# One VectorE instruction instead of two for the low parts of four chunks of a pair group

## The reference

```python
x = x + 0.5 * _swiglu(_rmsnorm(x, ffn1_norm), w_gate1, w_up1, w_down1)
u = _rmsnorm(x, mix_norm) @ w_in            # attention of two kinds on u
x = x + concat([a_out, b_out]) @ w_out
x = x + 0.5 * _swiglu(_rmsnorm(x, ffn2_norm), w_gate2, w_up2, w_down2)
x = _rmsnorm(x, final_norm)

def _swiglu(x, w_gate, w_up, w_down):
    return (silu(x @ w_gate) * (x @ w_up)) @ w_down
```

## Time and profile before

| | |
|---|---|
| median of three runs | 1835.73 us |
| the profiled execution, its own time | 1836.09 us |
| its span, first to last instruction | 1834.0 us |
| mean granted TensorE clock | 0.997 |
| TensorE matmul busy | 1819.8 us (99%) |
| TensorE weight load busy | 1511.5 us (82%) |
| VectorE busy | 1268.5 us (69%) |
| ScalarE busy | 922.6 us (50%) |
| GpSimd busy | 21.6 us (1%) |

### The profile page before, as it was taken

The page is one execution under the profiler, slowest core; times in us unless marked ns, Lnnn a source line. Parts: engine busy times, 40 slices in busy tenths (PEclk is TensorE's granted clock), DMA queues, the critical chain, the costliest instruction groups (busy, mean ns, idle before and its releaser), DMA issues.

```text
span 1834.0 us, 22446 instructions
## 1 busy us (share of the span) xinstructions
PE 1819.8 (99%) x8356; PEld 1511.5 (82%) x8356; DVE 1268.5 (69%) x1473; ACT 922.6 (50%) x1148; POOL 21.6 (1%) x19
## 2 busy tenths in 40 slices
PE   9999999999999999999999999999999999999998
PEld 7888888887888888888888888888888888888887
DVE  7888555887456868666666566888545887656865
ACT  7554434554344545554666445554434554344554
POOL 0000000000000000100000000000000000000000
PEclk9999999999999999999999999999999999999998
DMA  9565655556655657655554466565655556565653
GB/s 337 199 216 195 216 185 190 197 196 229 217 188 169 223 170 240 215 167 171 169 188 161 156 221 230 200 214 196 216 190 185 197 196 243 203 220 195 220 171 113
DMA packets 233792, 366.99 MB, mean 200 GB/s; under 512 B 16240, under 2 KB 94832, under 8 KB 233712
## 3 DMA queue, kind: packets, MB, share of 16 engines
q1 hardware_dynamic: 232224, 364.05, 59.4%
q10 hardware_dynamic: 1488, 1.87, 0.3%
HBM read 346.85 MB, written 2.10 MB: 190 GB/s over the span
## 4 chain that ended last, share of the span: by engine, by line
PE 95%; DVE 2%; DMA 1%; SPq 1%; ACT 0%; issue 0%; POOL 0%; DVEq 0%; ACTq 0%
PE psum L1804 74%; PE psum L1845 8%; PE psum L1717 7%; PE psum L1722 3%; DVE w_split L1189 1%; SPq L463 0%; DMA w_raw<-in_ffn_gate 0%; DMA w_raw<-in_ffn_down 0%; DMA w_raw<-in_ffn_up 0%; DVE strip_sum L1231 0%; DVE squares L1223 0%; PE psum L1964 0%; PE psum L1975 0%; PE psum L2010 0%; PE psum L1990 0%
## 5 line engine op out<-in xcount | busy, mean ns | idle before, releaser
L1804 PE MATMUL psum<-w_split,x_split 128*128 128x512 f32 x3984 | 915.9, 390 | 0.5 <-DVE w_split L1048 0.5
L1804 PEld LDWEIGHTS psum<-w_split,x_split 128*128 128x128 f32 x3984 | 746.9, 188 | 157.8 <-DVE w_split L1048 1.3
L606 ACT ACTIVATE w_split<-w_raw 128x1024 fp32r<-128x1024 f32 (+1 forms) x404 | 416.3, 1043 | 463.7 <-PE psum L1804 394.3
L1048 DVE TENSOR_TENSOR w_split<-w_raw,w_split 128x1024 fp32r<-128x1024 f32 (+1 forms) x404 | 477.7, 1203 | 241.7 <-ACT w_split L606 239.8
L1804 PE MATMUL psum<-w_split,h_split 128*128 128x512 f32 x2208 | 503.7, 390 | 1.6 <-DVE w_split L1189 1.2
L1804 PEld LDWEIGHTS psum<-w_split,h_split 128*128 128x128 f32 x2208 | 413.8, 188 | 89.7 <-DVE w_split L1189 2.6
L717 ACT ACTIVATE w_split<-w_raw 128x1024 fp32r<-128x1024 f32 (+1 forms) x320 | 319.3, 1013 | 280.8 <-PE psum L1804 189.9
L1189 DVE TENSOR_TENSOR w_split<-w_raw,w_split 128x1024 fp32r<-128x1024 f32 (+1 forms) x320 | 362.1, 1162 | 75.0 <-ACT w_split L717 73.8
L1845 PE MATMUL psum<-w_split,pair_sums 128*128 128x512 f32 x384 | 102.4, 395 | 0.0
L1845 PEld LDWEIGHTS psum<-w_split,pair_sums 128*128 128x128 f32 x384 | 72.1, 188 | 17.4
L1717 PE MATMUL psum<-x_split,w_split 128*128 128x512 f32 x256 | 79.9, 396 | 0.0
(11 more groups left out here) (211 smaller groups left out, 905.4 us busy)
## 6 DMA issues: line engine op xcount, KB each, us to landing
w_raw<-in_ffn_down SPq DMA_DIRECT2D x76, 1024.0 KB, 5.6
w_raw<-in_ffn_up SPq DMA_DIRECT2D x71, 1024.0 KB, 5.4
w_raw<-in_ffn_gate SPq DMA_DIRECT2D x70, 1024.0 KB, 5.4
w_raw<-in_w_in SPq DMA_DIRECT2D x48, 512.0 KB, 5.1
w_raw<-in_w_in SPq DMA_DIRECT2D x24, 1024.0 KB, 5.2
w_raw<-in_ffn_gate SPq DMA_DIRECT2D x34, 512.0 KB, 4.0
w_raw<-in_ffn_up SPq DMA_DIRECT2D x32, 512.0 KB, 4.8
w_raw<-in_w_out SPq DMA_DIRECT2D x16, 1024.0 KB, 5.4
```

Source lines behind the costliest of these rows:

```text
L606: nc.scalar.activation(w_split[:, slot % 2, 0, h * half:(h + 1) * half], w_raw[:, slot, h * half:(h + 1) * half], ACT.Copy).then_inc(hi_ma ...
L1048: nc.vector.tensor_tensor(w_split[:, slot % 2, 1, part], w_raw[:, slot, part], w_split[:, slot % 2, 0, part].bitcast(F32), ALU.subtract).t ...
L1804: ins = mm(psum[:, bank + t, :], x[:, a, t * P:(t + 1) * P], w[:, b, k, :], start=kk == 0 and (a, b) == (0, 0) and t in begins, stop=kk == ...
```

## The change

Inside `seven_low`, for jobs 8 to 11, the loop over two halves is replaced by one wait for the second half's high copy and one subtraction over all of the chunk (2048 elements; 1536 in the third part of the second stage for jobs 10 and 11, where the chunks are smaller). It adds 2 to `lo_made` when it ends. Jobs 2 to 7, the high copies, and all waits of other engines are as before.

```diff
                 kind, raw = SEVEN_JOBS[n]
                 c, slot, half = seven_base(ph, i) + n, raw % 4, kn * STRIP // 2
+                if n >= 8:
+                    dve.wait_ge(hi_made, hi_value(c, 1))
+                    nc.vector.tensor_tensor(w_split[:, n % 2, 1, 0:2 * half], w_raw[:, slot, 0:2 * half],
+                                            w_split[:, n % 2, 0, 0:2 * half].bitcast(F32), ALU.subtract).then_inc(lo_made, 2)
+                    return
                 for h, part in enumerate((slice(0, half), slice(3 * half // 2 if kind == "blocks" else half, 2 * half))):
                     dve.wait_ge(hi_made, hi_value(c, h))
                     nc.vector.tensor_tensor(w_split[:, n % 2, 1, part], w_raw[:, slot, part], w_split[:, n % 2, 0, part].bitcast(F32),
                                             ALU.subtract).then_inc(lo_made, 1)
```

## The result

The changed kernel takes 1861.81 us (median of 4 runs, 1861.6 to 1862.01) against 1835.9 us before (median of 4 runs too): a ratio of 1.0141, 95% interval [1.0128, 1.0154], 25.9 us slower. The forecast was 1861.8.

The account below looks back on a forecast made before the run. The matmul engine, busy 99%, was taken as the bound, VectorE mattering only by when it hands over chunks. Added waits of 22.5 + 3.2 + 0.5 - 0.1 = 26.1 us gave 1861.8 us; range 1857 to 1866, widened to 1853 to 1867.

Parts of the forecast that it names:

- VectorE's time is worth nothing: Matmul engine busy 99%, VectorE 69%: saved VectorE time gains nothing; only when it hands TensorE a chunk matters.
- The duration: One wide subtraction of 2048 elements on VectorE takes 2.285 us, against 2.36 for two halves.
- The chain of job 8, gates, silu and job 9: In each pair group gates and silu come 0.88 us late; TensorE waits 1.41 on average for job 9, 22.5 in all.
- Jobs 10 and 11: Job 10 covered by 2.4 us; job 11 at ends of parts 1 and 2: three groups 3.2 us, the fourth 0.5.
- Part 3's ends: In part 3's last groups the hidden columns TensorE waits for come 0.07 us earlier, twice: -0.1 us.
- the sum: All terms together, 22.5 + 3.2 + 0.5 - 0.1: 26.1 us slower, 1861.8 us on the median.
- B: Rival, 6%: gates not pushed, only the direct wait for the whole of job 9 counts, plus the ends: 1847.8 us.
- C: Rival, 3%: the granted clock falls to 1.2 GHz after some stalls, one plain job per pair group at half speed: 1948 us.
- D: Rival, 3%: the wide instruction is cheap, 2048 elements running at a higher rate than 1024; nothing slower, 1834 to 1836 us.
- E: Rival, 4%: unseen cover makes TensorE's waits shorter than the chain says; within 0.2%, about 1837 us.

Follow-up runs that it names:

- e11: Kernel before, with part-3 hidden columns first, half of job 11 ahead of the ups (but one group), jobs 8 to 10 wide, job 9's copy before silu: 1833.76 us.
- e5_job11: Kernel before, with only job 11's low part as one wide instruction: 1839.30 us, ratio 1.0019.
- e7_silu_last: Changed kernel, with the second high half of job 9 moved ahead of silu on ScalarE: 1838.98 us, ratio 1.0018.
- e3_jobs89: Kernel before, with the low parts of jobs 8 and 9 wide, jobs 10 and 11 in halves: 1858.83 us, ratio 1.0131.
- e4_job10: Kernel before, with only job 10's low part as one wide instruction: 1836.67 us, ratio 1.0004.
- e2_job9: Kernel before, with only job 9's low part as one wide instruction: 1843.37 us, ratio 1.0042.

## Why the prediction was right, step by step

**VectorE's time is worth nothing.** Right, by the changed kernel and by e11.

**The duration.** 2.285 us was forecast by the line through two shapes; 2.288 came (2.25 to 2.29). The Trainium skill's formula, page "VectorE: DVE Perf Modes", gives 2.29 too; the trace agrees.

**The chain of job 8, gates, silu and job 9.** Right, and shown from four sides: job 8 alone 0, job 9 alone 8.0, both 23.4, and nothing left of it with silu moved. The gates were forecast 4.6 us after job 7's first load and came at 80.31 - 75.67 = 4.64; silu 7.8, came 7.88. The wait was forecast with 1.41 on average. The sixteen add up to 26.05 us as the profile gives idle time; each holds the 0.04 us that always lies between two loads, so 1.59 each. 0.14 of that are the two starts of a wide instruction 0.07 later than I had put them. But the loads behind a wait run closer, 72 of them in 16.19 to 16.23 us where the same 72 take 16.28 without one, so that the net is the 1.53 us above. 16 x 1.53 = 24.4 us, forecast 22.5. What did not come as written is the order of the groups: the one at 1480 us was to have the smallest wait, 1.25, and has 1.70; the smallest, 1.42, is at 1201 us. How far ahead of the gates job 7 starts goes by the landing of the transfer that job 8's high copy waits for: in the group at 1480 us this copy starts 0.04 us after job 7's first load before, and 0.29 after. So the average carried over, and the single group did not.

**Jobs 10 and 11.** Right: three waits of 1.40 (forecast 0.34 + 1.07 = 1.41), the fourth 2.10 (1.63 + 0.5). The four idle times grow by 3.7 us, as forecast; less the up to 0.09 that TensorE regains behind each, the four ends together come 3.3 us later. The weight loads at the first end:

```profile
188.45 11.68 PEld L1809 LDWEIGHTS psum<-w_split,h_split 128*128 128x128 f32 x52 [1.40 <-DVE w_split L1189]
```

**Part 3's ends.** 3.0 us instead of 3.2, as forecast.

**What failed in the sum.** I wrote that no idle time of TensorE follows that could take the waits up. Inside a group that holds. But at the part ends before there were three waits for the moved hidden columns, 1.4 us together, which I had not counted since the profile lays them to "issue"; in the changed kernel they are gone. They are gone in both experiments with a wide job 11 at the part ends too (e5_job11, e7_silu_last), and stand at 1.4 and 1.8 us where job 11 is in halves (e3_jobs89, e4_job10): the longer wait for job 11 gives these columns time. So the waits for the low parts came to 24.4 + 3.3 = 27.7 us where I had 26.2, but the last group's job 9 starts only 26.5 us later than before, and from there to the end of the program the changed kernel is 0.7 us quicker, which leaves the 25.8 of the span. Of the 0.7, 0.5 lie between the mean of squares and the last scaling of the output: 2.24 us before, 1.74 after, with a granted clock in the last stretch of 0.66 where it was 0.52. In the trace of before the clock has fallen to 1.2 GHz ahead of the program's last eight weight loads, in an idle time of TensorE of 1.1 us: they take 1.78 us there, and 0.97 in the changed kernel, where it falls behind them. The windows (same columns as the earlier trace rows), before and after:

```profile
1824.00:1834.00 10.00, 2.07 (x8) 1.78 (x8) 3.94 (x6) 0.38 (x1) 2.46 (x2) 0.52 0.55 210
```

```profile
1850.00:1859.80 9.80, 1.19 (x9) 0.97 (x8) 4.10 (x7) 0.69 (x2) 2.51 (x2) 0.66 0.57 214
```

That the median agrees with the forecast to 0.01 us is therefore chance: errors of 1 to 2 us cancel. Two terms that no edit here touches also move between executions. The stretch of 2.24 us at the end stands in two of the 13 traces (before and e2_job9), and the other 11 have 1.74. The weight loads for the first norm start at 43.53 to 44.15 us in the 13 traces, at 43.88 before and 43.62 after.

**The rivals.** B (only the direct wait, 1847.8) falls by the gates' start and by e2_job9, which is B made real: 1843.4, 8.0 us for its part, forecast 8.5. C falls: twenty waits of up to 2.1 us, and the granted clock is 1.00 in every window of the changed kernel up to 1846 us, also around the wait of 2.10 at 452.90 (a window of the changed kernel, columns as in the earlier trace rows):

```profile
440.00:470.00 30.00, 28.32 (x123) 23.05 (x124) 18.50 (x19) 12.94 (x14) 0.00 (x0) 1.00 0.77 275
```

The prediction says beside C that its trace has no case of the half clock brought back by idle gaps; the nearest to one, which it passed over, is the fall ahead of the last eight loads, told above. D falls by the 2.288 us, and E by the twenty waits. The sentence of the Trainium skill, page "Perfetto Trace Analysis", section "Optimizing Scalar/DVE Operations", that broken-up instructions may let work be completed sooner where the engine is not saturated, is what this case shows: the same 2048 elements in two pieces are worth 25.9 us.

## What to carry to other kernels

Merging two instructions moves two moments, the start (all inputs must be there) and the release (one, at the end), and on an engine that is 69% busy these decide, not the 0.07 us saved. A merged instruction is free as long as the first consumer's demand is later than the end of the whole; work that out per place, and follow the queue behind it too, since a merge that is free alone (job 8) can raise the price of another further down the chain (8.0 us to 23.4). Where such a chain passes through a queue that orders unrelated work (silu ahead of a copy that needs nothing of it), moving that one entry can give back most of the loss, here 22.4 of 25.9 us.

## What the runs showed of the hardware that I had not expected

A subtraction of 2048 elements starts 0.10 us after the copy that releases it, in all 47 places of the changed kernel where it waits for one; one of 1024 or fewer starts after 0.03 us, in all places of the kernel before. The one of 1536 elements that waits has 0.10 too. And TensorE regains 0.05 to 0.09 us after a wait: 72 weight loads behind one take 16.19 to 16.23 us, without one 16.28.
